# Two matmuls in place of three in a feed-forward's gate and up products: a 512-column matmul over the activation's high and low halves

## The reference

```python
def swiglu(x, w_gate, w_up, w_down):                 # first block; the second has w_gate, w_up side by side
    return (jax.nn.silu(x @ w_gate) * (x @ w_up)) @ w_down

# first block, for each of 2 layers (D_FF = 2816)
x = layer_norm(ALPHA * x + 0.5 * swiglu(x, ffn1...), ...)
x = layer_norm(ALPHA * x + mixer(x), ...)            # pooling, convolution, neighbourhood attention
x = layer_norm(ALPHA * x + 0.5 * swiglu(x, ffn2...), ...)
# second block, for each of 2 layers
x = x + 0.5 * rmsnorm(swiglu(rmsnorm(x, ng[0]), w_ffn_in[l, 0], w_ffn_out[l, 0]), ng[1])
x = x + rmsnorm(mixer(rmsnorm(x, ng[2])), ng[3])     # three recurrent or attention branches
x = x + rmsnorm(mem_attn(rmsnorm(x, ng[4]), ...), ng[5])
x = x + 0.5 * rmsnorm(swiglu(rmsnorm(x, ng[6]), w_ffn_in[l, 1], w_ffn_out[l, 1]), ng[7])
```

## Time and profile before

| | |
|---|---|
| median of 3 runs | 3204.77 us (3203.74 to 3206.39) |
| span of the profiled execution | 3208.1 us |
| mean granted TensorE clock | 0.949 of full |
| PE, DVE, ACT, POOL busy | 90%, 54%, 38%, 31% |
| matmuls, each with a weight load | 24324 |
| read from HBM | 431.55 MB |

### The profile page before, as it was taken

The page is one execution under the profiler, slowest core; times in us unless marked ns, Lnnn a source line. Parts: engine busy times, 40 slices in busy tenths (PEclk is TensorE's granted clock), DMA queues, the critical chain, the costliest instruction groups (busy, mean ns, idle before and its releaser), DMA issues.

```text
span 3208.1 us, 58808 instructions
## 1 busy us (share of the span) xinstructions
PE 2874.5 (90%) x24324; PEld 2747.0 (86%) x24324; DVE 1724.1 (54%) x2153; ACT 1207.8 (38%) x1718; POOL 987.5 (31%) x436
## 2 busy tenths in 40 slices
PE   7989999898999899898679989989989867998998
PEld 7987899898789889777678888989977767888898
DVE  5556455556645566542855624665644284562465
ACT  3335344334544343322213444334432221344443
POOL 0025300002530000276845652000026684565200
PEclk9999999899999999998889999999999888999999
DMA  6664465565346456532212544655653221243463
GB/s 205 183 158 125 132 181 153 151 183 155 115 142 181 142 158 181 150 92 83 86 54 84 148 119 139 182 144 161 185 149 92 79 87 54 89 144 116 143 181 114
DMA packets 662818, 434.78 MB, mean 136 GB/s; under 512 B 27568, under 2 KB 638032, under 8 KB 662160
## 3 DMA queue, kind: packets, MB, share of 16 engines
q1 hardware_dynamic: 662672, 432.66, 46.5%
HBM read 431.55 MB, written 1.05 MB: 135 GB/s over the span
## 4 chain that ended last, share of the span: by engine, by line
PE 78%; DVE 11%; issue 5%; POOL 3%; ACT 3%; DMA 0%; SPq 0%; DVEq 0%; POOLq 0%; ACTq 0%
PE ps L349 22%; PE ps L350 21%; PE ps L351 21%; PE ps L525 3%; POOL w_lo L759 2%; PE ps L546 2%; DVE arena L1400 2%; DVE rstd L859 1%; PE ps L570 1%; DVE xT L884 1%; PE ps L1289 1%; DVE in_lo L809 1%; PE ps L1003 1%; PE ps L1096 1%; PE ps L1279 1%
## 5 line engine op out<-in xcount | busy, mean ns | idle before, releaser
L349 PE MATMUL ps<-in_hi,w_hi 128*128 128x256 f32 x4736 | 1382.0, 292 | 208.1 <-DVE in_lo L809 68.4
L350 PE MATMUL ps<-in_lo,w_hi 128*128 128x256 f32 x4736 | 1363.2, 288 | 0.0
L351 PE MATMUL ps<-in_hi,w_lo 128*128 128x256 f32 x4736 | 1362.0, 288 | 0.0
L349 PEld LDWEIGHTS ps<-in_hi,w_hi 128*128 128x128 f32 x4736 | 932.8, 197 | 233.2 <-issue 82.1
L759 POOL TENSOR_TENSOR w_lo<-raw,w_hi 128x1024 fp32r<-128x1024 f32 x284 | 705.9, 2491 | 1079.3 <-ACT w_hi L587 1069.7
L587 ACT ACTIVATE w_hi<-raw 128x1024 fp32r<-128x1024 f32 x682 | 719.2, 1055 | 725.2 <-PE ps L351 715.7
L350 PEld LDWEIGHTS ps<-in_lo,w_hi 128*128 128x128 f32 x4736 | 933.5, 197 | 0.8 <-issue 0.5
L351 PEld LDWEIGHTS ps<-in_hi,w_lo 128*128 128x128 f32 x4736 | 932.6, 197 | 0.0
L759 DVE TENSOR_TENSOR w_lo<-raw,w_hi 128x1024 fp32r<-128x1024 f32 x504 | 617.1, 1225 | 559.5 <-ACT w_hi L587 559.4
L349 PE MATMUL ps<-hid_hi,w_hi 128*128 128x256 f32 x1408 | 398.9, 283 | 0.7 <-DVE w_lo L759 0.7
L350 PE MATMUL ps<-hid_lo,w_hi 128*128 128x256 f32 x1408 | 398.4, 283 | 0.0
(11 more groups left out here) (299 smaller groups left out, 2920.7 us busy)
## 6 DMA issues: line engine op xcount, KB each, us to landing
raw<-in_w_ffn_in SPq DMA_DIRECT2D x176, 512.0 KB, 4.1
raw<-in_w_mix SPq DMA_DIRECT2D x112, 512.0 KB, 3.7
raw<-in_ffn_w_gate SPq DMA_DIRECT2D x88, 512.0 KB, 3.8
raw<-in_ffn_w_up SPq DMA_DIRECT2D x88, 512.0 KB, 3.8
raw<-in_ffn_w_down SPq DMA_DIRECT2D x88, 512.0 KB, 3.6
raw<-in_w_ffn_out SPq DMA_DIRECT2D x88, 512.0 KB, 4.4
raw<-in_w_in SPq DMA_DIRECT2D x40, 512.0 KB, 4.4
raw<-in_w_out SPq DMA_DIRECT2D x32, 512.0 KB, 4.4
```

Source lines behind the costliest of these rows:

```text
L349: nc.tensor.matmul(o, lh, rh, start=first, stop=False, **kw)
L350: nc.tensor.matmul(o, lh, rl, start=False, stop=False, **kw)
L351: return nc.tensor.matmul(o, ll, rh, start=False, stop=last, **kw)
```

## The change

The activation's two halves now lie in one tile, `in_both`, high and low side by side for each k. A matmul with the weights' high part takes both at once, 512 columns, into a whole PSUM bank; its left half is high·high, its right half high·low. A second matmul, 256 columns, adds low·high into the right half. Gate and up of a tile have a bank each, so a tile has two banks: 4 and 5 for even tiles, 6 and 7 for odd ones.

The two halves of a bank are added on the way out: ACT copies the left halves of both banks to SBUF (`gate_up_part`), DVE adds the right halves to them into `gate_up`, and in the second block DVE then scales by `rstd` in a separate step. SiLU and `hidden` read `gate_up` in both blocks. SiLU moves behind the split on ACT; `hidden` moves ahead of the low part on DVE except for the first tile, where it moves behind it. Two of the RMS statistics move to bank 0, and PE waits for `x_ready` 11 before the second block's second FFN. The down products and all other products stay as they are.

```diff
-        in_hi, in_lo = (sb(n, [P, KD, S], F32R) for n in ("in_hi", "in_lo"))
+        in_both = sb("in_both", [P, KD, 2, S], F32R)
+        in_hi, in_lo = (in_both[:, :, i, :] for i in range(2))
...
+        gate_up_part = work[:, 8 * S:12 * S].rearrange("p (j a t) -> p j a t", j=2, a=2)
...
-        FFN_BANK = (7, 4)
+        FFN_BANKS = (slice(4, 6), slice(6, 8))
+
+        def gate_up_bank(j, i):
+
+            return ps[:, FFN_BANKS[j % 2], :][:, i, :]
+
+        def gate_up_half(j, half):
+
+            return ps[:, FFN_BANKS[j % 2], half * S:(half + 1) * S]
+
+        def one_and_both(bank, w, k, first, last):
+
+            hi, lo = w
+            nc.tensor.matmul(bank.rearrange("p (a t) -> p a t", a=2), hi[:, k, :], in_both[:, k, :, :], start=first,
+                             stop=False, skip_group_check=True)
+            return nc.tensor.matmul(bank[:, S:2 * S], lo[:, k, :], in_hi[:, k, :], start=False, stop=last,
+                                    skip_group_check=True)
...
                         for k in (2 * c, 2 * c + 1):
-                            mm = three(ps[:, FFN_BANK[i // 2], i % 2 * S:(i % 2 + 1) * S], at2(w, ALL, k, ALL),
-                                       at2(given, ALL, k, ALL), k == 0 and i % 2 == 0, k == KD - 1, skip_group_check=True)
+                            mm = one_and_both(gate_up_bank(0, i), w, k, k == 0, k == KD - 1)
...
                     for k in range(KD):
-
-                        mm = three(ps[:, FFN_BANK[j % 2], i * S:(i + 1) * S], at2(w, ALL, k, ALL), at2(given, ALL, k, ALL),
-                                   k == 0, k == KD - 1)
+                        mm = one_and_both(gate_up_bank(j, i), w, k, k == 0, k == KD - 1)
...
         def act_ffn(act, n, e0, end, first=None):
 
 
+            def gate_up_taken(e, up, it):
+
+                act.wait_ge(sem("piece_used"), e0 + e + 1 + it * RAW)
+                nc.scalar.activation(gate_up_part[:, up % 2, :, :], gate_up_half(up, 0), ACT.Copy)\
+                    .then_inc(sem("gate_up_part"), 1)
+
+            def silu_of(j, it):
+
+                act.wait_ge(sem("gate_up_whole"), n * TILES + j + 1 + it * 2)
+                nc.scalar.activation(silu[:, j % 2, :], gate_up[:, j % 2, 0, :], ACT.Silu).then_inc(sem("silu_ready"), 1)
+
             def after(e, up=None, whole=None, it=0):
                 if up is not None:
+                    gate_up_taken(e, up, it)
                     if up == 0 and first is not None:
                         first()
-
-                    if first is not None:
-                        act.wait_ge(sem("gate_up_scaled"), n * TILES + up + 1 + it * 2)
-                        gate = gate_up[:, up % 2, 0, :]
-                    else:
-                        act.wait_ge(sem("piece_used"), e0 + e + 1 + it * RAW)
-                        gate = ps[:, FFN_BANK[up % 2], 0:S]
-                    nc.scalar.activation(silu[:, up % 2, :], gate, ACT.Silu).then_inc(sem("silu_ready"), 1)
+                if whole is not None and up is None:
+                    silu_of(whole, it)
                 if e0 + e + SPLIT < end:
                     act_split(act, e0 + e + SPLIT, it)
+                if up == 0:
+                    silu_of(0, it)
...
+            def gate_up_summed(j, it):
+
+                count = n * TILES + j + 1 + it * 2
+                dve.wait_ge(sem("gate_up_part"), count)
+                ins = nc.vector.tensor_tensor(gate_up[:, j % 2, :, :], gate_up_half(j, 1), gate_up_part[:, j % 2, :, :], ALU.add)
+                if first is not None:
+                    ins.then_inc(sem("gate_up_summed"), 1)
+                    dve.wait_ge(sem("gate_up_summed"), count)
+                    ins = nc.vector.tensor_tensor(gate_up[:, j % 2, :, :], gate_up[:, j % 2, :, :], over_two(rstd[:, :]),
+                                                  ALU.mult)
+                ins.then_inc(sem("gate_up_whole"), 1)
...
             def after(e, up=None, whole=None, it=0):
-                if up is not None and first is not None:
-                    if up == 0:
-                        first()
-                    dve.wait_ge(sem("piece_used"), e0 + e + 1 + it * RAW)
-
-                    nc.vector.tensor_tensor(gate_up[:, up % 2, :, :], two_tiles(FFN_BANK[up % 2]), over_two(rstd[:, :]),
-                                            ALU.mult).then_inc(sem("gate_up_scaled"), 1)
-                if up == 0:
-
+                if up == 0 and first is not None:
+                    first()
+                if up is not None:
+                    gate_up_summed(up, it)
+                if up is None and whole is not None:
                     hidden(whole, it)
                 if e + SPLIT < FFN_PIECES:
                     low_part(dve, e0 + e + SPLIT, it)
-                if up is None and whole is not None:
-                    hidden(whole, it)
+                if up == 0:
+                    hidden(0, it)
...
-        RMS_BANK = (6, 6, 7, 2, 0, 1, 0, 6, 6)
+        RMS_BANK = (0, 6, 7, 2, 0, 1, 0, 0, 6)
...
                 pe_rms(pe, 6)
+
+                pe.wait_ge(sem("x_ready"), 11)
                 pe_ffn(pe, 1, E_FFN2, C_FFN2, lambda: pe_rms(pe, 7))
```

More of the change, by code:

```diff
@@ L387, in gate_up @@
                 for i in range(2):
-                    if 2 * j + i < TOGETHER:
-                        continue
                     e = e0 + max(3 * j - 1, 0) + i
@@ L825, in hidden @@
                 dve.wait_ge(sem("silu_ready"), count)
-                up_part = ps[:, FFN_BANK[j], S:2 * S] if first is None else gate_up[:, j, 1, :]
-                nc.vector.tensor_tensor(hid[:, j, :], silu[:, j, :], up_part, ALU.mult)\
+                nc.vector.tensor_tensor(hid[:, j, :], silu[:, j, :], gate_up[:, j, 1, :], ALU.mult)\
                     .then_inc(sem("hidden_whole"), 1)
```

## The result

The changed kernel takes 3223.35 us, median of 4 runs (3221.90 to 3228.62), against 3204.26 us (3200.93 to 3206.39) for the kernel before on the same chip: a ratio of 1.0059, 95% interval 1.0045 to 1.0074. It is 0.6% slower. Forecast were 3156.3 us and a range of 3122 to 3192, so both the sign and the range were missed. The profiled execution has a span of 3226.8 us against 3208.1.

What follows compares the result with a forecast made beforehand. TensorE's matmul count times spacing was taken to bound the FFN stages; 66.1 us gained minus 17.6 us of losses gave 48.5 us off 3204.8, so 3156.3 us, range 3122 to 3192.

Steps and rivals of the forecast that it cites:

- columns alone: Rival for gate/up matmuls: columns set the spacing, removing a load gains nothing, only losses remain; 3222.4 us, chance 0.13.
- I take 216 ns: Gate/up in the FFNs: a 512-column matmul's stream hides the load; 24 ns less per triple, 66.1 us off.
- a fixed 13.3 ns per pair: Rival for gate/up: each load-and-matmul pair costs 13.3 ns beside its columns; gain 36.7 us, 3185.7 us, chance 0.28.
- The 256-column pair that follows still costs 120: Gate/up: the short matmul after the 512-column one stays at 120 ns, making a triple 336 ns.
- Last tile of FFN 1 in the first block: SiLU behind a split awaiting a late transfer delays the last down piece: 4.5 us x 2 layers, 9.0 us lost.
- The half clock for the last down piece: Bound on the FFN 1 last-tile loss, first block: idle time costs down(21) its clock, 2.9 us on top of 4.5.
- The other losses: Stage ends, first tiles and x_ready: 4.0, 0.6 (first block's second FFN), 2.4 and 0.8 (first tiles), 0.8 us.
- last tile, second block: Copy, add, scaling, SiLU and hidden make the last down piece wait: 1.0 us x 4 stages, 4.0 us lost.
- the x_ready wait: Before the last FFN PE waits for the residual holding banks 4 and 5: 0.4 us x 2, 0.8 us lost.
- No wait in the middle of a stage: Mid-FFN, the added ACT copy and DVE add are covered; the rival mid-stage wait and others had chance 0.05.
- At half clock 427 and 213 ns: Start of FFN stages: at half clock only columns count, spacing 427 and 213 ns, nothing gained.

Runs made afterwards that it cites:

- 4: Changed kernel with both gate/up matmuls at 512 columns in 20 of a stage's 22 tiles (another product): 3474.32 us, spacing 227.5 ns.
- 7: Changed kernel with two 384-column matmuls per triple for gate and up in 20 of 22 tiles (another product): 3204.48 us, spacing 173.5 ns.
- experiment 3: Changed kernel with the 512-column matmul taken apart into two of 256, a load each: 3241.51 us, ratio 1.0108 to the kernel before.
- 6: Changed kernel with each piece's eight long matmuls before its eight short ones, and the last tile's SiLU ahead of the split: 3186.84 us, ratio 0.9944.
- 9: Kernel of 6 with the gate piece taking its short matmuls first and the up piece its long ones: 3178.89 us, ratio 0.9921.

## Why the prediction was wrong

It foresaw -66.1 + 17.6 = -48.5 us. The runs have -18.2 + 37.3 = +19.1 (by the FFN stages in the traces, -16.8 + 35.2 = +18.4). The measured time lies 1 us from the rival "columns alone", 3222.4; that is luck, since this rival had a gain of 0 and losses of 17.6.

- **"I take 216 ns": the step that failed first.** It was worth 66.1 us and gave 18.2: the 512-column matmul took 235.9 ns to the next start. The argument was that the 13.3 ns beside the columns are a load showing from behind too short a stream. It leaned on two rows where the load is not to be seen: half clock with the same type, and fp32 at full clock. Neither shows this type at full clock with a longer stream; experiments 4 and 7 do, and the 13.3 ns stay. The rival "a fixed 13.3 ns per pair" was right in its number for a uniform stream, and its 36.7 us of gain would still have been double what came. It had also been said that the earlier trace rows fit it as well; that should have given it at least an equal chance. Its picture of one feed fits the half price of half the weights, but was only argued.
- **"The 256-column pair that follows still costs 120".** Right to 3 ns (116.9), but the mix of two lengths, out of this tile, costs some 6 ns a triple beyond 346.7, 6 x 2755 = 17 us. No rival had it. Alternation alone, the walk over k and the weights' tile are excluded as its cause, the activation's tile has to do with it, and more isn't known.
- **"Last tile of FFN 1 in the first block", 9.0 us.** This was the edit called the one that a reader misses, and its mechanism is what the trace shows: SiLU behind a split that waits for a late transfer. But undoing it gives back 27.6 us. The hidden part's 1.2 us were taken from undisturbed rows, while the split that is now ahead releases GpSimd at the same moment; the three instructions took 5.3 us, so PE's starts lay 8.0 and 8.5 us apart (idle 7.8 and 8.2), not 4.5. The half clock for the last down piece, given as a bound (2.9 us), came as well. And the same order stands in the second block's first FFN, where only the added steps had been counted: 5.0 us from start to start each (idle 4.7), in place of 1.0.
- **The other losses.** Forecast 4.0 (last tile, second block) + 0.6 + 2.4 + 0.8 + 0.8 = 8.6 us; what is left of 37.3 without 27.6 is 9.7 (by the FFN stages 35.2 - 29.4 = 5.8, and 1.2 of the x_ready wait, which lies ahead of a stage). Stage against stage, the second FFNs of experiment 3 are 0.55 us longer than before in the first block and 1.2 to 1.3 in the second, of 0.5 and 1.6 forecast. With SiLU moved, the second block's last tiles cost 1.3 us each against 1.0, the first block's second FFN 0.6 in place of 0.3, and the x_ready wait is there with 0.6 us a layer, against 0.4.
- **What was right.** No wait in the middle of a stage: ACT's copy takes 0.60 us and DVE's add 0.69, 176 times, and PE waits for neither. At half clock 427 and 213 ns. The added work is hidden there as worked out.

## What to carry to other kernels

Before paying for longer matmuls, measure one uniform stream of the length and type in question: on this kernel a load-and-matmul pair with 128 weight columns costs 13.3 ns beside its columns with F32R whatever the length of the stream, and 3 with bf16, and neither half clock nor another type tells it. Then measure the mix itself out of the real tile: here it cost 6 ns more than its parts. When an instruction is moved behind one that releases other engines, price what comes after it with those engines running: here a 0.4 us step became 2.4, at the end of each of the four first FFNs. And look at every place where the moved order occurs; the last tile of a loop that hands over to the next stage is where it costs, and undoing it there alone was worth 27.6 us and turned a loss into a gain.

## What the hardware showed beyond what was expected

- F32R pairs at full clock take the columns plus 13.3 ns (120, 173.5, 227.5 ns for 256, 384, 512), 6.8 with 64 weight columns; at half clock (1.2 GHz) nothing on top (213 and 427).
- F32R in two lengths by turns out of a tile with rows of 16 KB takes 353 ns, out of a small tile 347, and 348 with 128 bytes between the eight parts of the first.
- DVE's 256-column multiply and cast go from 0.42 and 0.29 us to 2.44 and 2.31 when GpSimd's subtraction of 1024 columns runs beside them.
- The first block's mixer, with the same matmuls in 6 and 9, took 144.8 to 150.7 us in their profiled executions, with 40 to 79 matmul starts at half clock: a difference of a few us between two single executions need not come from the edit.
